# Second attention of a fused block kernel: where the next head's turns, the third weight split and a few clears stand, and scores over 128 rows

## The reference

```python
def latent_attention(h, pos, w_in, q_norm, kv_norm, w_uq, w_ukv, q_gain, k_gain, w_out):
    c = h @ w_in
    c_q, c_kv, k_rope = jnp.split(c, [Q_LORA, Q_LORA + KV_LORA], axis=-1)
    q = (rmsnorm_2(c_q, q_norm) @ w_uq).reshape(B, S, B_HEADS, dqk)            # 16 heads of 96
    kv = (rmsnorm_2(c_kv, kv_norm) @ w_ukv).reshape(B, S, B_HEADS, QK_NOPE + V_DIM)
    ...
    q = rmsnorm_2(q, q_gain); k = rmsnorm_2(k, k_gain)     # then rotary embedding on the last 32
    def attend(args):
        s = jnp.einsum('bqhd,bshd->bhqs', q_blk, k).astype(jnp.float32) * scale
        s = jnp.where(key_idx[None, :] <= q_idx[:, None], s, NEG)
        p = jax.nn.softmax(s, axis=-1).astype(v.dtype)
        return jnp.einsum('bhqs,bshd->bqhd', p, v)
    ...
    return o @ w_out
```

## Time and profile before

| | us |
|---|---|
| median of 3 runs | 2672.14 |
| profiled execution | 2672.14 |
| its span in the trace | 2670.8 |
| PE busy | 2642.5 (99%) |
| DVE busy | 1435.9 (54%) |
| ACT busy | 982.7 (37%) |
| POOL busy | 319.5 (12%) |
| mean granted TensorE clock | 0.997 |

### The profile page before, as it was taken

How to read it: one execution, slowest core, us unless ns; L and a number is a source line. 1 busy time by engine, 2 the same in 40 slices (tenths; PEclk the granted TensorE clock), 3 DMA queues, 4 the chain that set the end, 5 groups by cost and what they waited for, 6 DMA issues and landing times.

```text
span 2670.8 us, 31302 instructions
## 1 busy us (share of the span) xinstructions
PE 2642.5 (99%) x12784; PEld 2216.1 (83%) x12784; DVE 1435.9 (54%) x2254; ACT 982.7 (37%) x1622; POOL 319.5 (12%) x388
## 2 busy tenths in 40 slices
PE   9999999999999999999999999999999999999999
PEld 8898888888887788779988888888888888888887
DVE  7637447565767444356874343453434676543433
ACT  4343334342454222236642222422223586422221
POOL 0000010000021000015530000100000586200000
PEclk9999999999999999999999999999999999999999
DMA  5322225523223444464323322233232101232321
GB/s 161 125 82 82 98 89 167 176 79 110 77 97 95 107 103 95 99 109 108 108 95 108 97 96 87 87 110 95 95 97 86 56 17 48 90 100 95 103 94 56
DMA packets 280936, 258.94 MB, mean 97 GB/s; under 512 B 40261, under 2 KB 275800, under 8 KB 280792
## 3 DMA queue, kind: packets, MB, share of 16 engines
q1 hardware_dynamic: 280775, 256.93, 32.4%
q10 hardware_dynamic: 16, 0.00, 0.0%
HBM read 242.23 MB, written 14.68 MB: 96 GB/s over the span
## 4 chain that ended last, share of the span: by engine, by line
PE 91%; DVE 4%; ACT 3%; issue 2%; POOL 1%; POOLq 0%; DVEq 0%; ACTq 0%
PE bank L1163 29%; PE bank L1165 29%; PE bank L1164 29%; PE bank L1321 1%; DVE Wl L1886 1%; POOL Wl L2446 0%; PE bank L1374 0%; PE bank L1174 0%; ACT Wh L1522 0%; PE bank L1470 0%; DVE Pl L2401 0%; POOL TMP L2453 0%; DVE Z L2393 0%; PE bank L1262 0%; DVE Hl L2358 0%
## 5 line engine op out<-in xcount | busy, mean ns | idle before, releaser
L1163 PE MATMUL bank<-Hh,Wl 128*128 128x512 f32 x2136 | 838.3, 392 | 1.8 <-DVE Hl L1905 1.8
L1165 PE MATMUL bank<-Hh,Wh 128*128 128x512 f32 x2136 | 832.1, 390 | 0.0
L1164 PE MATMUL bank<-Hl,Wh 128*128 128x512 f32 x2136 | 831.9, 389 | 0.0
L1886 DVE TENSOR_TENSOR Wl<-RAW,Wh 128x1024 fp32r<-128x1024 f32 (+2 forms) x420 | 493.7, 1219 | 161.9 <-ACT Wh L1522 161.1
L1522 ACT ACTIVATE Wh<-RAW 128x1024 fp32r<-128x1024 f32 (+2 forms) x454 | 441.1, 1022 | 363.1 <-PE bank L1165 337.3
L1163 PEld LDWEIGHTS bank<-Hh,Wl 128*128 128x128 f32 x2136 | 401.4, 188 | 88.1 <-DVE Hl L1905 3.1
L1163 PE MATMUL bank<-Ph,Wl 128*128 128x512 f32 x1200 | 470.9, 392 | 0.8 <-DVE Wl L1886 0.4
L1165 PEld LDWEIGHTS bank<-Hh,Wh 128*128 128x128 f32 x2136 | 401.4, 188 | 84.1
L1164 PEld LDWEIGHTS bank<-Hl,Wh 128*128 128x128 f32 x2136 | 401.6, 188 | 83.9 <-issue 1.7
L1165 PE MATMUL bank<-Ph,Wh 128*128 128x512 f32 x1200 | 467.3, 389 | 0.0
L1164 PE MATMUL bank<-Pl,Wh 128*128 128x512 f32 x1200 | 466.8, 389 | 0.0
(11 more groups left out here) (336 smaller groups left out, 2424.7 us busy)
## 6 DMA issues: line engine op xcount, KB each, us to landing
RAW<-in_ffn_wg SPq DMA_DIRECT2D x44, 1024.0 KB, 5.4
RAW<-in_ffn_wu SPq DMA_DIRECT2D x44, 1024.0 KB, 5.3
RAW<-in_ffn_wd SPq DMA_DIRECT2D x32, 1024.0 KB, 5.1
RAW<-in_w_up SPq DMA_DIRECT2D x22, 1024.0 KB, 5.1
RAW<-in_w_in SPq DMA_DIRECT2D x20, 1024.0 KB, 5.1
RAW<-in_ffn_wd SPq DMA_DIRECT2D x16, 768.0 KB, 4.4
bias_scratch<-M SPq DMA_DIRECT2D x16, 512.0 KB, 8.1
RAW<-in_w_down SPq DMA_DIRECT2D x8, 1024.0 KB, 5.2
```

Of the source, the lines that this page charges most:

```text
L1163: mm(o, ll, rh, start=start, stop=False)
L1164: mm(o, lh, rl, start=False, stop=False)
L1165: return mm(o, lh, rh, start=False, stop=stop)
L1886: tt(Wl[:, n % 3, x:y], RAW[:, n % 2, x:y], f(Wh[:, n % 3, x:y]), ALU.subtract).then_inc(*w_lo.up(*([("w_lo", n)] if i else [])))
```

## The change

In the loop the turns of q and k of head i + 1 now stand before the scores of head i. The attended head's eviction (`attended`) now stands before the units of its iteration, which was after them. The third `bg` tile's split and load stood ahead of the first unit of iteration 0, because `next_tile` looked one tile ahead there; it looks ahead only from group 4 on now, and one `split` and one `load` stand behind `b_sum` of iteration 2. DVE's sum of squares of unit (1, 0) moves behind its copy of q of head 0. Scores multiply all 128 rows of the slots where they took 96; for this a new step `b_rows` has POOL clear rows 96 to 127 of the two q slots (4 and 6) of `Hh` and `Hl`, after the last read of those slots as input, and scores wait for it once.

```diff
     def unit(g, u, ring=None):
         if (u, g % 2) == (2, 0):
-            tile[g // 2] = next_tile("bg", g // 2, 1 if g else 0)
+            tile[g // 2] = next_tile("bg", g // 2, 1 if g > 2 else 0)
...
     latent(1, n)
     do("used", n)
+    do("b_rows")
     for u in (2, 3):
         unit(1, u)
...
     head_qk(0, 0)
+    do("b_unit_sum", 1, 0)
     unit(1, 1)
...
             do("b_pt_lo", t, 0)
+        if i < 15:
+            for e in range(2):
+                head_qk(i + 1, e)
         for part in range(3) if i < 16 else ():
             scored.take(("b_s", i, part))
             do("b_scores", i, part)
...
         if t in (14, 15):
             do("b_pt_lo", t, 1)
-        if i < 15:
-            for e in range(2):
-                head_qk(i + 1, e)
...
             do("b_exp", i, 1)
             do("b_sum", i)
+        if i == 2:
+            split()
+            load()
+        if v >= 0 and v % 2:
+            attended(v // 2)
         if 2 <= i < 12:
             for u in (0, 1) if i % 2 else (2, 3):
                 unit(g, u)
-        if v >= 0 and v % 2:
-            attended(v // 2)
...
+                pe.wait_ge(*at("b_rows"))
                 for n, z in PARTS_B[part]:
                     L, qs = 128 * (n + 1), slice(128 * n, 128 * n + 128)
-                    mm(o[:, z:z + L], ql[0:96, qs], kh[0:96, 0:L], start=True, stop=False)
-                    mm(o[:, z:z + L], qh[0:96, qs], kl[0:96, 0:L], start=False, stop=False)
-                    ins = mm(o[:, z:z + L], qh[0:96, qs], kh[0:96, 0:L], start=False, stop=True)
+                    mm(o[:, z:z + L], ql[:, qs], kh[:, 0:L], start=True, stop=False)
+                    mm(o[:, z:z + L], qh[:, qs], kl[:, 0:L], start=False, stop=False)
+                    ins = mm(o[:, z:z + L], qh[:, qs], kh[:, 0:L], start=False, stop=True)
...
-                if (g, u) in ((0, 0), (0, 1)) and kind == "b_unit":
+                if (g, u) in ((0, 0), (0, 1), (1, 0)) and kind == "b_unit":
...
+            elif kind == "b_rows":
+                pool.wait_ge(*at(("b_c", 1)))
+                pool.wait_ge(*at(("b_ks", 0)))
+                memset(f(Hh[96:128, 4:7:2, :]), 0.0).then_inc(*pool_out.up("b_rows_hi"))
+                pool.wait_ge(*at("b_rows_hi"))
+                memset(f(Hl[96:128, 4:7:2, :]), 0.0).then_inc(*pool_out.up("b_rows"))
+                pool.wait_ge(*at("b_rows"))
```

More of the change, by code:

```diff
@@ L665, in order @@
     now["low"] = "pool"
-    attend_b_order(banks, tmps, next_tile, norm_step, hkeys, h_new, h_pair, stats, add_x, do)
+    attend_b_order(banks, tmps, next_tile, split, load, norm_step, hkeys, h_new, h_pair, stats, add_x, do)
     now["low"] = "dve"
@@ L809, in attend_a_order, with attend_b_order @@
     out_units(32)
-def attend_b_order(banks, tmps, next_tile, norm_step, hkeys, h_new, h_pair, stats, add_x, do):
+def attend_b_order(banks, tmps, next_tile, split, load, norm_step, hkeys, h_new, h_pair, stats, add_x, do):
     do("b_begin")
```

## The result

| | before | after |
|---|---|---|
| median us (range, runs) | 2671.52 (2670.05 to 2672.7, 4) | 2685.61 (2685.38 to 2686.53, 4) |
| profiled execution | 2672.14 | 2686.53 |
| its span | 2670.8 | 2685.2 |
| mean granted clock | 0.997 | 0.995 |

The change makes the kernel slower: ratio 1.0054, 95% interval 1.0041 to 1.0067. The forecast was 2688.1 (2669 to 2702), 2.5 us above the median and 1.6 above the profiled execution.

A forecast was written before the change was run, and what follows sets the result against it. PE is busy 99% of the span, so time counts only where PE lacks an instruction or runs at the lower clock. From 2672.14: less 0.14 (start), plus 7.1 (pairs) and 9.0 (clock), giving 2688.1 us, range 2669 to 2702.

The forecast's parts named there:

- What must be ready for the moved turns: Odd iterations: moved turns wait for the k/v units' `Pl` copies to free banks 0 and 1, iteration 7's at 2182.1.
- The pairs: Iterations 4/5, 6/7, 8/9, 10/11: each loses 1.77 us, 7.1 in all, bounds 0.3 to 10.4.
- The start: Loop's start up to iteration 4: 0.14 us saved, bounds 1.5 saved and 1.06 lost.
- The gate: Iteration 3: head 4's turns need POOL's scaling of group 2, so k turns start at 2145.05.
- The clock: PE falls to half clock in holes of iterations 3, 5 and 9: three falls at 3.0, 9.0 us lost, bounds 0 to 23.
- Rows: Score matmuls over 128 rows instead of 96: priced at 0, bounds 0.1 us either way per head.
- Rival C: The working for the pairs holds but the clock never falls, perhaps because all 128 rows work: 2679.1 us, chance 0.2.
- The Trainium skill's variant: Transposes do not guard the clock, so iterations 7 and 11 fall too: 6 us more, about 2694.
- The clears: Two memsets on POOL, at most 4.2 us, hidden in its idle 2.37 and 3.88 us ahead of the norm steps.
- The hole of 2.57: PE's 2.57 us hole ahead of head 0's turns should go almost entirely; the wait only moves to head 4's turns.
- Rival A: No gain or loss: odd iterations swap their 1.06 us hole for an equal one, clock holds; 2672.3 us, chance 0.22.
- B: Rival, faster: turns find free banks, and four holes, the 2.57 and the clock's 4.6 go; 2660.7 us, chance 0.1.

The follow-up runs named there:

- fill_turns: after, with 24, 24, 16 and 28 unused 128x128 transposes before the moved turns of iterations 3, 5, 7 and 9; 2680.1 us, ratio 1.0032.
- fill: after, with 12, 12, 8 and 14 unused 128x512 matmuls before the moved turns of iterations 3, 5, 7 and 9; 2680.5 us, ratio 1.0032.
- rows_only: before, with only the scores over 128 rows and the clears added; 2671.2 us, ratio 1.0000.
- turns_back96: after, with the turns of the next head behind the scores again and scores over 96 rows; 2669.76 us, ratio 0.9995.

## Why the prediction came out right

**What must be ready for the moved turns.** Right. The releaser of every hole of the moved turns in iterations 3 to 11 is the `Pl` named, but for the second of 11 (POOL's `M`, 0.65 us). Counted from the start of iteration 6 in after (timelines of ACT and of DVE, after; their starts less 2176.43):

```profile
2181.24 0.72 ACT L1815 ACTIVATE Z<-Z,pkf 128x512 f32<-128x512 f32 x1 [1.63 <-DVE pkf L2399]
```

```profile
2179.07 1.41 DVE L2364 SCALAR_TENSOR_TENSOR Hl<-bank,sm,Hh 96x512 fp32r<-96x512 f32 x2 [0.36 <-ACT Hh L1805]
2180.39 0.80 DVE L2399 CUSTOM_DVE_ANT_0 Z<-bank,maskb,sm 128x512 f32<-128x512 f32 x1
...
2187.18 0.61 DVE L2357 SCALAR_TENSOR_TENSOR Pl<-bank,pkf,Ph 128x128 fp32r<-128x128 f32 x2 [0.33 <-ACT Ph L1796]
```

The first maximum begins 3.96 us in, behind both `Hl` copies (2.20 in the earlier trace rows; I said 1.87 later, it is 1.76). ACT now idles 1.63 us for it, against 1.00 in the earlier trace rows. The last `Pl` ends at 11.36; the prediction's 2182.1 is 11.3. Iteration 7 then took 12.80 us instead of 9.75. One slip: the prediction has 1.14 us for the q/k copies in its bound on ACT, where the earlier trace rows say 1.24; the 1.2 that it took does not hang on it.

**The pairs.** Forecast 1.77 each; with the clock held up (fill_turns) 1.61, 1.64, 1.60 and 1.65. In after they lost 2.6, 3.0, 4.0 and 1.7 (4/5, 6/7, 8/9, 10/11): the first three hold what the clock took besides, the last had no fall. From iteration 12 on nothing is added, as priced. Start and pairs together: 6.7 for 7.0.

**The start.** 0.14 saved was forecast. Iteration 4 began 0.19 later in fill_turns, 1.4 later in after, with a fall ahead of it. The gate was half right: head 4's first turns wait for `Pl` of the units, held up on ACT by the moved split; POOL's `M` comes behind it and ends last only where PE is at full speed (2145.73 in fill_turns, for the 2145.05 worked out). POOL's chain for head 4 ended 0.7 us sooner than before, counted from the loop's start, and not 1.2.

**The clock.** This is the term that was mis-sized: 9.0 forecast, 12.7 - 6.7 = 6.0 by the loops of after and fill_turns, 5.1 by the medians of after and fill. Falls came in 3, 5 and 9 as forecast, and in 7 and not 11, one of the two left in doubt. There were four falls at some 1.5 us each, where three at 3.0 were forecast. That price came from the 4.6 us that before's fall seemed to cost; rows_only puts that one at 0.9, since without it PE waits behind it for `Hl` and for `M`.

**Rows.** Priced at 0: right for matmul durations and for a loop with short holes (turns_back96), wrong in this one, where the edit to 96 rows costs 5.2 us in the median. Rival C named 128 rows as what might keep the clock up. It is true in part: they shorten the falls and do not prevent them. With the clock held up by other work, in fill_turns, the kernel took 2680.1 for C's 2679.1: C had the pairs right and the clock wrong.

**The sum.** Against the profiled execution the clock was 3.0 us too much, start and pairs 0.3 too much, and the fall of 1.7 us outside the loop was not in it: 2686.5 for 2688.1. So the closeness is luck in part: for the loop alone 16.0 us were forecast and 12.7 measured, and a fall that nobody forecast, in code that the change does not touch, made up half of the difference.

**The Trainium skill's variant**, 2694 with falls in 7 and 11, failed on fill_turns and on iteration 11.

**The clears.** Hidden, as said: 0.95 us each, from 2111.67 to 2113.62, and POOL idled 0.36 and 3.81 us ahead of the norm steps behind them, where the earlier trace rows have 2.37 and 3.88 (POOL, after):

```profile
2113.98 0.21 POOL L2555 TENSOR_TENSOR pkf<-pkf 128x8 f32<-128x8 f32 x1 [0.36 <-DVE pkf L2349]
```

**The hole of 2.57** went, and iteration 2 began 2.65 us sooner, counted from the loop's start (13.25 for 15.90). It did not shorten the loop, as said: behind it PE waited 1.68 and 1.07 us at turned pieces and then 3.19 at head 4's gate.

**Rival A** fell on the holes themselves, and **B** on 14.8 us of waits where it had none.

## What to carry to other kernels

Before a step is moved to an earlier place in an in-order queue, look for the last writer that frees its destination bank and compare that end with the new place; copies that move with it push back everything behind them on the other engines, and copies that stay behind make new waits. Here either way cost some 1.6 us in each of four pairs of iterations. A hole and a clock fall are two prices, and they are told apart by filling the hole with unused work. Slow matmuls in front of a wait for another engine cost little (0.9 us of 4.6 here), so the cost of a fall is read at the next wait and not from its length.

## What the runs showed of the hardware that was not expected

- The number of contraction rows went with the clock: with the same first holes, score matmuls over 96 rows gave 37.5 us at half clock and over 128 rows (32 of them zeros) 20.5, in one execution each, and mean clocks of 0.992 to 0.994 against 0.995 and 0.996 in all. In the kernel before, ten of 21 executions were at 0.997, with 128 rows none of 11. Matmul durations did not differ (0.48 us for 512 columns in both kinds at full speed). Why is open, and so is the share of the clears that came with the 128 rows.
- Transposes (f32, 128x128) in the holes held the clock up as matmuls did (fill_turns: 0 us at half clock in the loop, after 20.5).
- In the loops of all these kernels falls came in lengths of 3.4, 6.8 and 10.2 us. The same pair of holes, 1.96 and 0.65 us, brought one in iteration 7 and none in 11 of the same execution; why is open. Which falls come also changes from one execution of a kernel to the next: before had mean clocks from 0.996 to 1.000.
